# Attention jobs of 64 queries of both heads of a pair on 128 partitions, the sample block as one job in four parts, in a new order

## What is computed

```python
def mla_attend(q_lat, q_rope, ckv, krope, mask):
    s = (jnp.einsum('bqhc,bkc->bhqk', q_lat, ckv, preferred_element_type=jnp.float32)
         + jnp.einsum('bqhr,bkr->bhqk', q_rope, krope, preferred_element_type=jnp.float32)) * SM_SCALE
    if mask is not None:
        s = jnp.where(mask, s, -jnp.inf)
    p = jax.nn.softmax(s, axis=-1).astype(ckv.dtype)
    return jnp.einsum('bhqk,bkc->bqhc', p, ckv)
```

## Time and profile before

| what | value |
|---|---|
| median of 3 runs (lowest, highest) | 2380.13 us (2379.26, 2382.15) |
| the profiled execution | 2377.99 us |
| its span, first to last instruction | 2375.8 us |
| TensorE products busy | 2006.6 us (84%), 16286 |
| VectorE busy | 950.8 us (40%), 1442 |
| ScalarE busy | 645.2 us (27%), 1257 |
| GpSimd busy | 203.3 us (9%), 287 |
| mean granted TensorE clock | 0.921 |

### The profile page before, as it was taken

How to read it: one execution, slowest core, us unless ns; L and a number is a source line. 1 busy time by engine, 2 the same in 40 slices (tenths; PEclk the granted TensorE clock), 3 DMA queues, 4 the chain that set the end, 5 groups by cost and what they waited for, 6 DMA issues and landing times. The chain is left out here.

```text
span 2375.8 us, 39464 instructions
## 1 busy us (share of the span) xinstructions
PE 2006.6 (84%) x16286; PEld 1755.2 (74%) x16286; DVE 950.8 (40%) x1442; ACT 645.2 (27%) x1257; POOL 203.3 (9%) x287
## 2 busy tenths in 40 slices
PE   5999963398888889979974399599999999999997
PEld 3999931166667657656662298499999999999996
DVE  4122147345344435534531811923333333333336
ACT  5223341123323323423421512521111111111114
POOL 0000000123223112313110000010000000000000
PEclk8999987599899979989986799899999999999998
DMA  7111045501000001000008330211110111101122
GB/s 264 43 44 44 18 123 130 175 16 43 17 32 28 17 17 31 30 17 20 4 6 284 135 119 27 102 36 54 54 45 21 43 54 54 45 20 44 54 102 75
DMA packets 112174, 147.75 MB, mean 62 GB/s; under 512 B 65968, under 2 KB 80944, under 8 KB 111568
## 3 DMA queue, kind: packets, MB, share of 16 engines
q1 hardware_dynamic: 112016, 145.41, 18.9%
HBM read 114.90 MB, written 30.50 MB: 61 GB/s over the span
## 5 line engine op out<-in xcount | busy, mean ns | idle before, releaser
L355 PE MATMUL ps<-hhi,whi 128*128 128x364 f32 (+1 forms) x1728 | 572.0, 331 | 73.3 <-DVE wlo L348 36.9
L355 PE MATMUL ps<-hlo,whi 128*128 128x364 f32 (+1 forms) x1728 | 571.4, 331 | 0.0
L355 PE MATMUL ps<-hhi,wlo 128*128 128x364 f32 (+1 forms) x1728 | 571.3, 331 | 0.0
L355 PEld LDWEIGHTS ps<-hhi,whi 128*128 128x128 f32 x1728 | 328.0, 190 | 74.9 <-issue 57.8
L355 PEld LDWEIGHTS ps<-hlo,whi 128*128 128x128 f32 x1728 | 327.9, 190 | 0.0
L355 PEld LDWEIGHTS ps<-hhi,wlo 128*128 128x128 f32 x1728 | 327.6, 190 | 0.0
L348 DVE TENSOR_TENSOR wlo<-wraw,whi 128x1024 fp32r<-128x1024 f32 x74 | 90.5, 1224 | 491.3 <-ACT whi L344 489.4
L667 POOL TENSOR_TENSOR nlev<-gm,con 64x256 f32<-64x256 f32 x204 | 153.3, 752 | 250.0 <-DVE gm L1255 236.0
L1488 DVE TENSOR_TENSOR acc<-acc,ps 128x364 f32<-128x364 f32 (+1 forms) x240 | 126.6, 531 | 101.9 <-PE ps L1907 101.8
L1907 PE MATMUL ps<-ahi,dhi 128*128 128x364 f32 (+1 forms) x480 | 158.5, 330 | 2.4 <-DVE acc L1488 2.4
L1907 PE MATMUL ps<-alo,dhi 128*128 128x364 f32 (+1 forms) x480 | 157.5, 328 | 0.0
(11 more groups left out here) (212 smaller groups left out, 2713.2 us busy)
## 6 DMA issues: line engine op xcount, KB each, us to landing
wraw<-in_w_tiles SPq DMA_DIRECT2D x72, 512.0 KB, 3.4
late<-in_ada_w SPq DMA_DIRECT2D x8, 2048.0 KB, 9.5
ci<-scan SPq DMA_DIRECT2D x17, 768.0 KB, 4.5
draw<-in_w_down SPq DMA_DIRECT2D x20, 512.0 KB, 3.4
slab<-in_ada_w SPq DMA_DIRECT2D x4, 2048.0 KB, 18.3
scan<-mix SPq DMA_DIRECT2D x12, 512.0 KB, 4.4
x<-in_x_t SPq DMA_DIRECT2D x4, 1456.0 KB, 9.8
x<-x_mid SPq DMA_DIRECT2D x1, 4352.0 KB, 13.3
```

What stands on the lines that cost most here:

```text
L355: mm = nc.tensor.matmul(ps[:, 3 * u + c, 0:n], w[u][:, k, :], x[:, k, a:a + n], start=(k == 0 and w is whi and x is hhi), stop=(k == KD - ...
```

## The change

- A job is now 64 queries of both heads: head 0 on partitions 0 to 63, head 1 on 64 to 127. The prompt has 16 such jobs, each with exactly the keys that its chunk sees, so the memset goes. Scores and values are products of 64 stationary columns that alternate between the heads.
- The sample is one job. Its 2112 keys are scored in four parts of 528, each with its own maximum, exponential and sum; the four are brought to one scale by a few operations on four columns (`S_SCALE`, `S_TOTAL`). Its probabilities have a buffer of their own (`spr`).
- The order is by hand: prompt jobs from 1024 keys to 64, the sample as the seventh, its parts scored with jobs 3 to 6 of the list. Turns hold up to four tiles (three for the sample), values stand one turn behind their turn, and `pt` is a ring of three. `put_out` comes with each job.
- The key projections of the next pair stand at the end of a pair, where no scores are left to be asked for.
- `interleave` now goes by the number of attention units on TensorE, no longer by columns: 100 units in a pair where there were 86. `before_small` (an increment of a semaphore that nothing waits for) stands ahead of scores, turns and values.

```diff
+PROMPT_JOBS = list(reversed(range(TP // C)))
+SAMPLE_JOB, SAMPLE_PARTS, SAMPLE_AT = TP // C, 4, 6
+SKEYS = TS + PAST
+SPART = SKEYS // SAMPLE_PARTS
+JOB_ORDER = PROMPT_JOBS[:SAMPLE_AT] + [SAMPLE_JOB] + PROMPT_JOBS[SAMPLE_AT:]
+JOBS = len(JOB_ORDER)
...
+def job_groups(job):
+
+    n, most = (job // 2 + 1, 4) if job < SAMPLE_JOB else (1 + PAST // P, 3)
+    parts = -(-n // most)
+    return [(n * i // parts, n * (i + 1) // parts) for i in range(parts)]
...
+TURNS = [(job, t0, t1) for job in JOB_ORDER for t0, t1 in job_groups(job)]
+T_END = {job: i + 1 for i, (job, _, _) in enumerate(TURNS)}
+SCORES = [(job, 0) for job in PROMPT_JOBS[:2]]
+for at, next_job in enumerate(PROMPT_JOBS[2:]):
+    SCORES += [(next_job, 0)] + [(SAMPLE_JOB, at)] * (at < SAMPLE_PARTS)
+S_END = {job: i + 1 for i, (job, _) in enumerate(SCORES)}
+P_END = {job: i + 1 + (SAMPLE_PARTS - 1) * (i >= SAMPLE_AT) for i, job in enumerate(JOB_ORDER)}
+N_SCORES, N_TURNS, N_NORMS, RING = len(SCORES), len(TURNS), P_END[JOB_ORDER[-1]], 3
+assert N_SCORES % 2 == 0 and N_TURNS % RING == 0
...
+def pair_units(first, last):
+
+    units = [("keys", l, 0) for l in range(len(K_CHUNKS)) if first]
+    units += [("query", l, 0) for l in range(2 * len(CH))] + [("value", g, 0) for g in range(len(V_GROUPS))]
+    next_keys = [("keys", l, 1) for l in range(len(K_CHUNKS)) if not last]
+    scored, out, before = 0, None, None
+
+    def scores(count):
+        nonlocal scored
+        new = range(scored, min(scored + count, N_SCORES))
+        scored += len(new)
+        units.extend(("scores", x, 0) for x in new)
+        if not new and next_keys:
+            units.append(next_keys.pop(0))
+        return [("exp", x, 0) for x in new]
+
+    units += scores(2) + [("norm", JOB_ORDER[0], 0)]
+    for i, job in enumerate(JOB_ORDER):
+        groups = [x for x, turn in enumerate(TURNS) if turn[0] == job]
+        for x in groups:
+            units.append(("turn", x, 0))
+            if out is not None:
+                units.append(("out", out, 0))
+                out = None
+            if x == groups[0]:
+                if i + 1 < JOBS:
+                    units.append(("norm", JOB_ORDER[i + 1], 0))
+                exps = [] if job == SAMPLE_JOB else scores(2 if i < SAMPLE_PARTS else 1)
+            if x == groups[-1]:
+                units += exps
+            if before is not None:
+                units.append(("values", before, 0))
+                if TURNS[before][0] != job:
+                    out = TURNS[before][0]
+            before = x
+    return units + [("out", out, 0), ("values", before, 0), ("out", JOB_ORDER[-1], 0)] + next_keys
+
+
+FIRST_UNITS, MID_UNITS, LAST_UNITS = pair_units(True, False), pair_units(False, False), pair_units(False, True)
+
+
+def unit_counts(units):
+
+    return [int(kind not in ("exp", "norm", "out")) for kind, _, _ in units]
+
...
+                if job == SAMPLE_JOB and part == SAMPLE_PARTS - 1:
+                    act.wait_ge(smp_max, hp + 1)
+                    nc.scalar.activation(sm[:, S_SCALE:S_SCALE + SAMPLE_PARTS], sm[:, S_NMAX:S_NMAX + SAMPLE_PARTS], ACT.Exp,
+                                         bias=sm[:, S_ALL:S_ALL + 1], scale=-1.0).then_inc(smp_scale, 1)
...
+            def put_probs(x, hp):
+
+                _, t0, t1 = TURNS[x]
+                at_least(act, o_mm, N_TURNS * hp + x - RING + 1 + 1)
+                act.wait_ge(t_mm, N_TURNS * hp + x + 1 + 1)
+                nc.scalar.copy(pt[:, x % RING, 0:P * (t1 - t0)], ps[:, 4, 0:P * (t1 - t0)]).then_inc(t_ev, 1)
 
...
+            def job_max(x, hp):
+                job, part = SCORES[x]
+                dve.wait_ge(s_mm, N_SCORES * hp + x + 1)
+                if job == SAMPLE_JOB:
+                    nc.vector.tensor_reduce(sm[:, S_NMAX + part:S_NMAX + part + 1], score_cols(x), mybir.AxisListType.XY, ALU.max,
+                                            negate=True).then_inc(nmax, 1)
+                    if part == SAMPLE_PARTS - 1:
+                        dve.wait_ge(nmax, N_SCORES * hp + x + 1)
+                        nc.vector.tensor_reduce(sm[:, S_ALL:S_ALL + 1], sm[:, S_NMAX:S_NMAX + SAMPLE_PARTS], AX_X, ALU.min).then_inc(smp_max, 1)
...
+            def job_norm(job, hp):
+                dve.wait_ge(p_exp, N_SCORES * hp + S_END[job])
+                if job == SAMPLE_JOB:
+                    scale = sm[:, S_SCALE:S_SCALE + SAMPLE_PARTS]
+                    sums = sm[:, S_SUM:S_SUM + SAMPLE_PARTS]
+                    dve.wait_ge(smp_scale, hp + 1)
+                    step.done(nc.vector.tensor_tensor(sums, sums, scale, ALU.mult))
+                    step.done(nc.vector.tensor_reduce(sm[:, S_TOTAL:S_TOTAL + 1], sums, AX_X, ALU.add))
+                    step.done(nc.vector.reciprocal(sm[:, S_RECIP:S_RECIP + 1], sm[:, S_TOTAL:S_TOTAL + 1]))
+                    step.done(nc.vector.tensor_scalar(scale, scale, sm[:, S_RECIP:S_RECIP + 1], None, ALU.mult))
+                    for part in range(SAMPLE_PARTS):
+                        keys = spr[:, SPART * part:SPART * part + SPART]
+                        nc.vector.tensor_scalar(keys, keys, sm[:, S_SCALE + part:S_SCALE + part + 1], None, ALU.mult).then_inc(p_norm, 1)
...
+            def put_out(job, hp):
+                a = C * job
+                dve.wait_ge(o_mm, N_TURNS * hp + T_END[job] + 1)
+                nc.vector.tensor_copy(oatt[:, bass.ds(hp, 1), a:a + C].rearrange("p a b -> p (a b)"), ps[:, 5, 0:C]).then_inc(o_ev, 1)
...
+            def scores(x, hp):
+
+                job, _ = SCORES[x]
+                q0 = TP if job == SAMPLE_JOB else C * job
+                if x >= 2:
+                    pe.wait_ge(p_exp, N_SCORES * hp + x - 1)
...
+                before_small()
+                for b, k0, n in score_pieces(x):
+                    for e in range(2):
+                        mm = nc.tensor.matmul(ps[64 * e:64 * e + 64, 2 * (x % 2) + b, 0:n], qt[e][0:96, q0:q0 + C], kt[e][0:96, k0:k0 + n],
+                                              start=True, stop=True)
                 mm.then_inc(s_mm, 1)
...
+            def turn(x, hp):
+
+                job, t0, t1 = TURNS[x]
+                pe.wait_ge(p_norm, N_NORMS * hp + P_END[job])
+                at_least(pe, t_ev, N_TURNS * hp + x)
+                before_small()
                 for t in range(t0, t1):
...
+                    _, k0, rows = tile_rows(job, t)
+                    mm = nc.tensor.transpose(ps[0:rows, 4, P * (t - t0):P * (t - t0) + P], probs_of(job)[:, k0:k0 + rows], ident)
                 mm.then_inc(t_mm, 1)
...
+            def values(x, hp):
+                job, t0, t1 = TURNS[x]
+                n = job_groups(job)[-1][1]
+                pe.wait_ge(t_ev, N_TURNS * hp + x + 1)
+                if t0 == 0:
+                    pe.wait_ge(o_ev, JOBS * hp + JOB_ORDER.index(job) + 1)
+                before_small()
+                for t in range(t0, t1):
+                    at, _, rows = tile_rows(job, t)
+                    for e in range(2):
+                        r = slice(64 * e, 64 * e + 64)
+                        mm = nc.tensor.matmul(ps[r, 5, 0:C], vt[0:rows, at, r], pt[0:rows, x % RING, P * (t - t0) + 64 * e:P * (t - t0) + 64 * e + 64],
+                                              start=(t == 0), stop=(t == n - 1))
+                mm.then_inc(o_mm, 1)
...
+            def keys(l, hp):
+                dst, n = K_CHUNKS[l]
+                if l == 0:
+                    pe.wait_ge(aw_in, 16 * hp + 16)
+                    at_least(pe, p_exp, N_SCORES * hp)
...
+            def query(l, hp):
+                e, (a, n) = l // 3, CH[l % 3]
+                if l == 0:
+                    at_least(pe, t_ev, N_TURNS * hp)
+                elif l == 1:
+                    pe.wait_ge(o_ev, JOBS * hp + 1)
```

More of the change, by code:

```diff
@@ L967, in put_probs, with attend_scalar @@
[L967 to L978 removed]
+            def attend_scalar(hp, units):
+                for kind, x, ahead in units:
+                    if kind == "keys":
+                        put_keys(x, hp + ahead)
+                    elif kind == "query":
+                        put_query(x, hp)
+                    elif kind == "value":
+                        put_value(x, hp)
+                    elif kind == "exp":
+                        exponentials(x, hp)
+                    elif kind == "turn":
+                        put_probs(x, hp)
+                    yield
@@ L1017, in _ @@
             split_hi(act, OUT_M, 1)
[L1020 removed]
+            act.wait_ge(o_ev, JOBS * PAIRS + 1)
             act.wait_ge(rw_done, KR)
@@ new lines, in attend_vector @@
+            def attend_vector(hp, units):
+                for kind, x, ahead in units:
+                    if kind == "keys":
+                        put_keys(x, hp + ahead)
+                    elif kind == "query":
+                        put_query(x, hp)
+                    elif kind == "scores":
+                        job_max(x, hp)
+                    elif kind == "norm":
```

(19 more changed lines are left out.)

338 lines of the change are left out of this document (112 added, 226 removed).

## The result

The changed kernel takes 2255.57 us (2253.61 to 2258.72, 4 runs) against 2379.7 us (2373.31 to 2382.15, 4 runs): a ratio of 0.9484, 95% interval 0.9462 to 0.9505. Forecast were 2250 us in a range of 2200 to 2315, and faster with a chance of 0.93. The profiled execution took 2253.6 us, its span is 2251.7 us at a mean clock of 0.939.

A forecast was written before the change was run, and what follows sets the result against it. TensorE was taken as the bound of the 796 us attention stage, with 106 us of waits. Gains of 75 - 5 + 46 + 12 = 128 us took 2378 to 2250 us, range 2200 to 2315.

The forecast's parts named there:

- Part 1: Attention lines on TensorE: alternating heads overlap in scores and values, cheaper sample turns; 75 us gained, 5 lost to further units.
- The 43 ns: Price per value record, taken from the scan's alternating heads: 1424 records at 62 us, a gain of 44 us.
- 75 - 5: Attention lines on TensorE: 75 us gained on scores, values and turns, less 5 us for 56 further units.
- comparison of 43 with 101 ns: Same product form in the trace: 43 ns a record in the alternating scan, 101 ns in the sample's lone-head values.
- rival 2: Scores of both heads don't overlap, values do: 87 of 128 us lost, 2337 us; chance 0.07.
- Part 3: Scan and turns at a pair's end run at the full clock: 3 us a pair, 12 us in all.
- upper end of 25: Largest clock gain allowed, 25 us, if the other low-clock stretches go too; 12 us was taken.
- Part 2: TensorE's waits in the attention stage fall from 106 to 60 us as the long sample block goes: 46 us gained.
- Rival 1: The waits only move: short jobs at a pair's end wait as long as the sample block did; 2308 us, chance 0.16.
- Rival 3: Nothing overlaps, neither scores nor values of the two heads: slower, 2419 us; chance 0.03.
- rival 4: Softmax chain laid bare, every job waits for its reduction through scaling: slower, waits of 189 us, 2391 us; chance 0.04.

## Why the prediction was right

- **Part 1, TensorE's time.** The mechanism is shown: products for different halves of the output partitions lie beside each other, also at 264 to 512 columns, which no row of before had. Prompt scores cost 91.5 - 17.4 = 74.1 us (forecast 71.8), sample scores 17.4 (15), turns 53.5 + 12.4 (53.4 + 12.6). Values cost 71.1 us instead of 62: that term was mis-sized by 9 us. The 43 ns came from the scan's units of 16 records. The timeline has values units of 4, 8, 12 and 16 records at 0.34, 0.45, 0.57 and 0.69 us, that is some 29 ns a record and 0.22 us a unit, so short units are dearer per record. Units with a tile of 64 keys take 0.10 to 0.15 us more, 4 us in all. The lines together gained 289.4 - 228.5 = 60.9 us, against 75 - 5 = 70. Not all of this is overlap: at the full clock the sample's eight score units would have taken 8 x 3.76 = 30.1 of their 37.7 us and its eight values units 8 x 2.31 = 18.5 of 27.4, so some 16 of the 60.9 us are the clock. The comparison of 43 with 101 ns, on which the prediction rested, set a full clock against a lower one; 43 against 68 ns is the fair one, and in the single records the step is 58 ns for one product record of a lone head or for one of each head. The overlap was real, and its proof partly luck.
- **The rule against the change.** The scores keep their overlap, although both heads use the same rows; rival 2 falls with the 183.6 and 91.5 us above. The Trainium skill, TensorE: Matmul & The Clock Gate, "Part 3: Packing small matmuls — row/col tiling", says of weight loads that they overlap running products only when their row group differs. This case's runs disagree: both heads share their rows, and 183.6 us with a wait between the heads are 91.5 without. But the rule is about loads, and the prediction took too much from it: the table of the same section has three products side by side in different column groups, 2.38 times as fast, and the two heads are such a case.
- **Part 3, the clock.** TensorE's other lines fell from 689.9 - 289.4 = 400.5 to 607.5 - 228.5 = 379.0 us with no record changed: 21.5 us, near my upper end of 25 and not the 12 I took. The stage's clock rose from 0.91 to 0.97; that all of the 21.5 us are the clock was not separated. The prediction had named a change outside the attention's lines as a sign against it; it came, on the cheap side. By luck this and the values' miss cancel: 60.9 + 21.5 = 82.4 us of busy time, forecast 82.
- **Part 2, the waits.** The size was right (47.5 us, forecast 46; 58.6 left, forecast 60), the attribution was not. I wrote that the waits before L1676, L1782 and L1797 "lose their cause" with the sample's long block. With the sample cut to 320 keys, the kernel before still waited 105.1 us. The values "one turn behind", to which I gave the 18.7 us before the transposes, are worth nothing either. "The next pair's seven key projections are put there as cover" was right, 23 us. What ended the scan's wait (22.0 to 2.1 us on `xt`) stays open: the scan is now laid between jobs by the count of units and not by their columns, and there are more and smaller units. An experiment with the old rule on the new units was not run.
- **"No instruction outside the stage changes"** was true of the work, but not of its time. The stage gained 130 us, the span 2375.8 - 2251.7 = 124.1. The 6 us between are outside: 9 lost behind the stage (see below) and 3 gained ahead of it, where it starts at 458 and not 461 us.
- **Rivals.** Rival 1 falls (58.6 us of waits, not 100). Rival 3 falls, and its price of 2419 us was too high: the kernel with the overlap mostly taken away takes 2356. Its scores cost 175.7 us, as priced (143.6 + 30), but its values 108.0 and not 144, since 101 ns was a price at the lower clock; and the waits shrink all the same. For rival 4, the transposes' wait for scalings is 9.5 us in all, in the first job of each pair.

## What to carry to other kernels

Where an output of 64 partitions leaves half the array unused, issue the two halves' products together and without a wait between them. Here a wait between the scores' halves cost 87 us. Half of one ahead of the other did no harm up to four records; longer runs of small products should alternate, and above all not go back and forth between 64 and 128 rows. Before comparing two prices, look at the granted clock in each. Judge such a packing by the busy time of the group, not by the mean length of a record, which is the same either way. Before blaming a stage's waits on its largest block, shrink the block and see whether they go.

## What the runs showed of the hardware

- Overlap does not need neighbours. With 4 records of a head ahead of the other's nothing was lost, neither with the scores (1.20 us against 1.19) nor with the values (0.46 against 0.45). With 6 and 8 of the small ones ahead, units of 12 and 16 records took 0.73 and 0.94 us, where they took 0.57 and 0.69. What limits the distance was not tried.
- A change of form costs about 0.1 us. In the single records of the changed kernel, at the full clock in this stage, the first product of a line starts 51 ns (median of 146) after the last of the line before it where both are 64*64, but 148 ns from 64*64 to 128*64 (92) and 152 from 128*64 to 128*128 (57). The rows of 1213 us, in which the prediction saw no gap, have this step too: the last record of L1713 starts at 1213.02 and the first of L1779 at 1213.17 us. A record lasts 0.22 us, so the two still overlap in the merged rows. So what a further unit costs is mostly its change of form.
- The feed-forward part lost time though its code is the same. The same engine view, groups by line in 300 us of it, before (1924 to 2224 us) and after (1800 to 2100 us):

```profile
L355 PE MATMUL ps<-hhi,whi 128*128 128x364 f32 (+1 forms) x387 | 127.9, 330 | 6.0 <-issue 6.0
L355 PE MATMUL ps<-hhi,wlo 128*128 128x364 f32 (+1 forms) x387 | 127.8, 330 | 0.0
L355 PE MATMUL ps<-hlo,whi 128*128 128x364 f32 (+1 forms) x387 | 127.8, 330 | 0.0
```

```profile
L391 PE MATMUL ps<-hhi,whi 128*128 128x364 f32 (+1 forms) x384 | 128.3, 334 | 5.6 <-issue 5.6
L391 PE MATMUL ps<-hlo,whi 128*128 128x364 f32 (+1 forms) x384 | 128.2, 334 | 3.1 <-issue 3.1
L391 PE MATMUL ps<-hhi,wlo 128*128 128x364 f32 (+1 forms) x384 | 128.0, 333 | 0.0
```

A second gap without a releaser appears in the loop (1.34 us at 1825 us, 3.1 us in this stretch), and the clock in these stretches is 0.98 after and 0.99 before. From the stage's end to the last instruction it is 1128 us after and 1119 before. Over the whole of that part the kernel before has 3 such gaps of 8.9 us on these lines, the changed kernel 6 of 13.2, and its variants with the full sample 6 of 13.0 to 14.0. With a short sample the changed kernel has 3 of 8.9 (1120 us for this part, with fewer instructions ahead of it), and with the keys at the start 6 of 11.4 (1124 us). Its cause was not tried.
